# Gate products of an mLSTM stage: their 544 columns cut as 512 and 32 instead of 272 and 272

## The reference, cut to what matters

```
p = (h @ w_in).astype(jnp.float32)                 # h: tokens x 1024, normed and modulated
q = p[..., :hk]
k = p[..., hk:2 * hk] * (DK_A ** -0.5)
...
gates = p[..., 2 * hk + 2 * D_MODEL:] + b_gates.astype(jnp.float32)
ig = gates[..., :H_A]
lf = jax.nn.log_sigmoid(gates[..., H_A:])
```

## Time and profile before

| | |
|---|---|
| median of 3 runs | 1377.57 us (1377.35 to 1378.26) |
| span of the profiled execution | 1376.5 us; no time of its own is given for it beside the span |
| PE (matmuls) | 1328.3 us busy, 96% of the span |
| PEld (weight loads, beside the matmuls) | 1291.6 us, 94% |
| DVE, ACT, POOL | 52%, 26%, 38% |
| mean granted clock of TensorE | 0.989 of full speed |

### The profile page before, as it was taken

How to read it: one execution, slowest core, us unless ns; L and a number is a source line. 1 busy time by engine, 2 the same in 40 slices (tenths; PEclk the granted TensorE clock), 3 DMA queues, 4 the chain that set the end, 5 groups by cost and what they waited for, 6 DMA issues and landing times.

```text
span 1376.5 us, 26372 instructions
## 1 busy us (share of the span) xinstructions
PE 1328.3 (96%) x11593; PEld 1291.6 (94%) x11593; DVE 720.0 (52%) x1124; ACT 362.4 (26%) x560; POOL 524.6 (38%) x248
## 2 busy tenths in 40 slices
PE   5899999999999999999999999999989999999997
PEld 4799889999899999999999999999989999999996
DVE  2714445677931541441548819759871551641774
ACT  3532443222421221221223333122321221211311
POOL 2433424433333333434334344434334444343440
PEclk9899999999999999999999999999999999999999
DMA  9675213654455446445442233223133323323321
GB/s 330 201 195 145 66 53 115 219 167 143 138 160 178 151 127 190 153 145 170 152 141 83 59 105 89 86 75 105 49 93 92 90 81 91 91 80 91 93 62 65
DMA packets 239804, 169.34 MB, mean 123 GB/s; under 512 B 5691, under 2 KB 211775, under 8 KB 239562
## 3 DMA queue, kind: packets, MB, share of 16 engines
q1 hardware_dynamic: 215946, 121.33, 29.9%
q10 hardware_dynamic: 23584, 46.27, 10.5%
q0 software_dynamic: 160, 0.07, 0.0%
HBM read 160.70 MB, written 6.94 MB: 122 GB/s over the span
## 4 chain that ended last, share of the span: by engine, by line
PE 82%; DVE 10%; issue 3%; ACT 2%; DMA 1%; POOL 1%; ACTq 0%; SPq 0%; POOLq 0%; DVEq 0%
PE G L1527 55%; PE G L1553 19%; PE B L1623 3%; DVE acc L997 1%; DVE hb L1120 1%; DVE small_s L1467 1%; DVE yc L1466 1%; DMA xin<-in_x_sample 1%; PE B L1813 1%; PE B L1513 1%; ACT wh L457 1%; DVE Xl L1134 1%; PE B L1815 1%; PE B L1885 1%; DVE sqb L959 1%
## 5 line engine op out<-in xcount | busy, mean ns | idle before, releaser
L818 POOL TENSOR_TENSOR wl<-raw,wh 128x1024 fp32r<-128x1024 f32 x192 | 483.9, 2523 | 684.9 <-ACT wh L457 681.9
L457 ACT ACTIVATE wh<-raw 128x1024 fp32r<-128x1024 f32 x192 | 202.8, 1057 | 475.7 <-PE G L1527 190.7
L1527 PE MATMUL G<-Xh,wh 128*128 128x272 f32 x960 | 205.5, 296 | 5.0 <-ACT stage L464 4.0
L1527 PE MATMUL G<-Xl,wh 128*128 128x272 f32 x960 | 199.4, 289 | 0.0
L1527 PE MATMUL G<-Xh,wl 128*128 128x272 f32 x960 | 198.3, 288 | 0.0
L1527 PE MATMUL G<-Hh,wh 128*128 128x272 f32 x864 | 180.2, 290 | 0.0
L1527 PE MATMUL G<-Hl,wh 128*128 128x272 f32 x864 | 178.6, 288 | 0.0
L1527 PE MATMUL G<-Hh,wl 128*128 128x272 f32 x864 | 177.5, 287 | 0.0
L1527 PEld LDWEIGHTS G<-Xh,wh 128*128 128x128 f32 x960 | 150.6, 190 | 11.0 <-issue 8.7
L976 DVE TENSOR_TENSOR small_s<-G,modT 128x32 f32<-128x32 f32 x80 | 15.2, 190 | 264.9 <-PE G L1527 202.9
L1527 PEld LDWEIGHTS G<-Xl,wh 128*128 128x128 f32 x960 | 152.0, 190 | 0.0
(11 more groups left out here) (324 smaller groups left out, 2021.9 us busy)
## 6 DMA issues: line engine op xcount, KB each, us to landing
aring<-in_ada_w ACTq DMA_DIRECT2D x78, 512.0 KB, 4.8
raw<-in_mlp_w_up SPq DMA_DIRECT2D x64, 512.0 KB, 4.0
raw<-in_mlp_w_down SPq DMA_DIRECT2D x64, 512.0 KB, 3.6
raw<-in_mlstm_w_in SPq DMA_DIRECT2D x24, 512.0 KB, 4.1
raw<-in_conv_w_in SPq DMA_DIRECT2D x24, 512.0 KB, 3.8
early<-in_ada_w SPq DMA_DIRECT2D x16, 512.0 KB, 12.4
raw<-in_mlstm_w_out SPq DMA_DIRECT2D x8, 512.0 KB, 5.3
raw<-in_conv_w_out SPq DMA_DIRECT2D x8, 512.0 KB, 3.6
```

The source lines that it names most:

```text
L457: nc.scalar.activation(wh[:, t % SLOTS], raw[:, t % RAWS], ACT.Copy).then_inc(s_hi, 1)
L818: nc.gpsimd.tensor_tensor(wl[:, t % SLOTS], raw[:, t % RAWS], wh[:, t % SLOTS].bitcast(F32), ALU.subtract).then_inc(s_lo, 1)
L1527: last = mm(G[:, 2 * (g % 2) + hf, 0:HALF], w[:, s, k, :], x[:, k, hf * HALF:(hf + 1) * HALF], start=st, stop=en)
```

## The change

The columns of the gate products are cut at 512: the first three matmuls of a step take columns 0 to 511 into bank B5, the next three take columns 512 to 543 into bank B7. The order changes with it: a bank's three products now stand together, where the two halves took turns. VectorE reads the banks by the same cut, two instructions of 512 columns and two of 32, into the same rows. The tiles of line 1527 keep their halves of 272.

```diff
--- before.py
+++ after.py
@@ -250,6 +250,7 @@
         rstd = B[:, 1:3, 0:HALF]
         SUMS = 500
         ada_out = B4[:, 0:KT * GW]
+        GATE_COLS = ((slice(0, SEQ), B5), (slice(SEQ, TOK), B7))
 
         def ada_tile(a):
             return aring[:, a % ADAS] if a >= ADA_RING else (early0 if a < 8 else early1)[:, a % 8]
@@ -1187,10 +1188,9 @@
             dve.wait_ge(s_gin, 80)
             R = [r[:, :] for r in rows]
             lf = sqb[0:H, :]
-            for hf, bank in enumerate((B5, B7)):
-                cols = slice(hf * HALF, (hf + 1) * HALF)
-                V.tensor_scalar(R[3][:, cols], bank[0:H, 0:HALF], bgate[0:H, :], None, ALU.add)
-                V.tensor_scalar(R[4][:, cols], bank[32:32 + H, 0:HALF], bgate[32:32 + H, :], None, ALU.add)
+            for cols, bank in GATE_COLS:
+                V.tensor_scalar(R[3][:, cols], bank[0:H, 0:cols.stop - cols.start], bgate[0:H, :], None, ALU.add)
+                V.tensor_scalar(R[4][:, cols], bank[32:32 + H, 0:cols.stop - cols.start], bgate[32:32 + H, :], None, ALU.add)
             chain.link(V.memset(xr[0:H, :], 1.0))
             V.scalar_tensor_tensor(R[0], R[4], -1.0, R[4], ALU.mult, ALU.max).then_inc(s_rv, 1)
             dve.wait_ge(s_ra, 1)
@@ -1703,9 +1703,9 @@
 
             def gates(k):
                 pe.wait_ge(s_kx, X_NORM0 + k + 1)
-                for w, x, st, en in ((gh, Xh, k == 0, False), (gh, Xl, False, False), (gl, Xh, False, k == KT - 1)):
-                    for hf, bank in enumerate((B5, B7)):
-                        last = mm(bank[0:40, 0:HALF], w[:, k, :], x[:, k, hf * HALF:(hf + 1) * HALF], start=st, stop=en)
+                for cols, bank in GATE_COLS:
+                    for w, x, st, en in ((gh, Xh, k == 0, False), (gh, Xl, False, False), (gl, Xh, False, k == KT - 1)):
+                        last = mm(bank[0:40, 0:cols.stop - cols.start], w[:, k, :], x[:, k, cols], start=st, stop=en)
                 if k == KT - 1:
                     last.then_inc(s_gp, 1)
```

## The result

The changed kernel takes 1379.62 us in the median of 18 runs (1378.49 to 1383.88), the kernel before 1377.75 us in 18 runs (1374.95 to 1380.83). The ratio is 1.0016, with a 95% interval of 1.001 to 1.0022: 2.2 us slower, 1.4 to 3.0. The forecast was 0.9 us slower, 1378.4 us, with a range up to 1380.0. The two medians alone lie 1.9 us apart. So sign and range hold, and the size is more than twice the one forecast. The profiled execution spans 1377.6 us, 1.1 us more than that of before.

The account below looks back on a forecast made before the run. TensorE was taken to bound the kernel, with six gate steps in the first tile on its path. Five at 2.4 GHz (0.58 us) plus one at 1.2 GHz (0.30 us) gave +0.88 us: 1378.4 us, range 1376.9 to 1380.0 us.

Parts of the forecast that it names:

- the operands of the gates are ready in time: First tile: the last two subtractions end at 53.69 us, so TensorE, now later, waits less for gate operands.
- The sum of the path: Gate steps inside the first weight tile on TensorE: five at 2.4 GHz and one at 1.2 GHz add 0.88 us.
- A step at 2.4 GHz: One gate step after 49.03 us: 866 ns against 750, 116 ns more; five such steps 0.58 us.
- The seam: From the last narrow gate product to the tile's next matmul: 111 ns for an exposed 128-column load; below 60 means wrong.
- The step at 1.2 GHz: The gate step k = 2 at 46.36 us: 1663 ns against 1363, 0.30 us more.
- nothing behind it should change: Stages after the first tile keep their times; a gain or loss above 0.2 us behind 64 us means wrong.
- a late rise: Rival in the first tile: exposed loads delay the rise to 2.4 GHz; 1385 us if low to the gates' end; chance 0.03.
- a rise at another moment: Rival near the gates: the clock rises at another time, moving the total 1 to 2 us either way; chance 0.06.
- The hidden wide load: Rival at the gate steps: the tile's weight load stays hidden, no difference, 1377.6 us; chance 0.24.
- Narrow products that wait for each other: Rival at the gate steps: each narrow product costs about 191 ns, 3.1 us more in all, 1380.7 us; chance 0.03.
- Wide matmuls cheaper than their columns: Rival at the gate steps: 512 columns cost only 125 ns, 1.1 us or somewhat more saved, 1376.4 us; chance 0.02.
- Two passes for each narrow product: Upper bound at the gate steps: narrow products run as two passes with own loads, 0.84 us more, +1.7 us in all.

Follow-up runs that it names:

- the third profile: The changed kernel run a third time without an edit, beside a copy of the kernel before: 1379.73 us, ratio 1.0012 to the kernel before.
- the delays: The kernel before with seven or fourteen extra matmuls of 272 columns in the third tile: 1381.82 us (1.0028) and 1382.97 us (1.0038).
- narrow first: The changed kernel with the three 32-column products ahead of the three of 512: 1378.89 us, 1.0012; as 35 spare steps in the kernel before, 1410.42 us.
- the order by turns: The kernel before with 35 spare gate steps, their products cut 512, 32, 512, 32, 512, 32: 1409.79 us, ratio 1.0234.

## Why the prediction was right or wrong

**The place and the sign** were right. The six gate steps inside the first tile lie on TensorE's path, the two ahead of it hide behind GpSimd (in the changed kernel the wait for it is still 1.10 us; it was to shrink by 0.3 us, and did so by 0.20, to 0.77, in the third profile, where the clock was low ahead of it as in the kernel before), and VectorE's reading costs the same: 2 x 0.74 + 2 x 0.24 = 1.96 us.

One premise held only in part: "the operands of the gates are ready in time" was read from one profile, and in three of nine TensorE waits for them, which takes most of the price away there.

**The sum of the path** was right: +0.88 us forecast, +0.85 in the pair of profiles with the clock alike, +0.80 (0.5 to 1.1) at equal clock over all runs, and +0.55 between the averages of all profiles. Its terms were off in both directions. A step at 2.4 GHz costs 0.14 us more, not 0.116. The wide ones are 230 ns and not 225, so the part over the columns is not a constant 11.7 ns but grows with them, to 17. The narrow ones are 35 ns and not 40. The load of 128 columns adds 90 ns to the pair behind it, beside the 40 ns to its start, 130 together, where I had 111. The seam itself, from the last narrow product to line 1527, is 40 ns, below the 60 that I had named as a sign of being wrong: the load costs what it should, but one pair further on. The step at 1.2 GHz was 0.30; the third profile has it at 47.37 - 45.89 = 1.48 us, with a first pair of 0.60 where 0.455 is the rule there, so 1.48 + 0.145 - 1.363 = 0.26 us.

**Wrong was the term for what comes behind 64 us**, "nothing behind it should change". I let the clock count only near the gates: a late rise with 0.03, and a rise at another moment "by chance" with 0.06 and in either direction. In the runs the mean clock is 0.001 lower with the change, which is 1.04 us, more than the path itself. That the change brings the lower clock is not shown; the delays speak for it, and the single profiles do not. I had read the clock only near the gates and not where TensorE waits later on. The profile of before had those stretches at 372 and 1000 us to be seen.

**The rivals.** The hidden wide load falls: narrow first is 0.07 us a step cheaper, which is that load. Narrow products that wait for each other fall by the order by turns, 0.141 against 0.137. Wide matmuls cheaper than their columns fall at 230 ns for 512 columns; that is also against the 131 ns of the Trainium skill, "TensorE: Matmul & The Clock Gate", section "Back-to-back issue gap". A clock that rises late in the first tile did not happen in any of the three profiles of the change: it rose 3.5, 3.7 and 4.1 us behind the tile's start, against 4.1 before. Two passes for each narrow product fall too, since each is one record and they start 30 to 40 ns apart.

**The slowdown** of 0.16% stays below the 0.2% that I had given as the least a measurement can tell, and the chances, 0.93 for within it, fit. The median of 18 runs missed mine by 1.2 us. The kernel before missed itself by as much once. That it still lies inside the range is luck: the upper end, 1380.0 us, stood there for two passes, which did not happen, and for a spread of runs that I took from three (0.9 us), where the kernel before scatters from 1374.8 to 1382.0 us.

## What to carry to other kernels

Cutting a matmul's columns unevenly changes neither the columns nor the count, but each narrow one uncovers the weight load behind it; put a wide one ahead of the widest load, and price the seam by rows with few columns. An average clock belongs in the record of each run: at equal clock 36 runs gave 0.80 us where the medians said 1.9. One profile of each kernel is not enough for a stage that can wait: here the first pair gave 0.56 us, and the nine pairs of three profiles each give anything from -0.42 to 0.85. Where TensorE waits and the clock falls behind it, a shift of about 1 us upstream went along with a microsecond or more downstream here, though why is open, so look at every such place, not only at the one that is edited.

## What was not expected of the hardware

The load behind the last narrow matmul is not seen as a gap ahead of the wide one: the first 128 x 272 starts 40 ns later, and it is its pair that stretches, from 0.25 to 0.34 us. The distance between wide matmuls exceeds the columns' time at 2.4 GHz by 11.7 ns for 272 columns and by 17 ns for 512, while at 1.2 GHz it is the columns' time in both (0.43 us for 512 in the third profile, 46.32 - 45.89). And 0.87 us of matmuls put into the kernel before cost 3.8 us, of which 0.9 us is a longer wait and some 1.5 us goes with the lower mean clock.
